# Row norms of a two-layer decoder trunk: turning by products with a diagonal of row scales instead of scaling and transposing

## The reference

```
def rms_norm(x, g):
    y = x * lax.rsqrt(jnp.mean(x * x, axis=-1, keepdims=True) + RMS_EPS)
    return y * g

mem_n = rms_norm(mem, mem_norm_g)
for layer in range(2):
    xn = rms_norm(h, norm_g[layer])
    mem_kv = mem_n @ mem_w_kv[layer]
    mixed = even_layer(xn, ...) if layer % 2 == 0 else odd_layer(xn, ...)   # begins with xn @ w_in
    h = h + mixed @ w_out[layer]
return rms_norm(h, final_norm_g)
```

## Time and profile before

| | before |
|---|---|
| median of 3 runs | 2272.27 us (2271.89 to 2274.04) |
| the profiled execution | 2272.63 us |
| its span in the profile | 2271.0 us |
| TensorE busy | 2232.5 us (98%) |
| VectorE, ScalarE, GpSimd busy | 1018.3, 821.7, 409.4 us |
| chain that ended last: TensorE | 96% |

### The profile page before, as it was taken

The page is one execution under the profiler, slowest core; times in us unless marked ns, Lnnn a source line. Parts: engine busy times, 40 slices in busy tenths (PEclk is TensorE's granted clock), DMA queues, the critical chain, the costliest instruction groups (busy, mean ns, idle before and its releaser), DMA issues.

```text
span 2271.0 us, 30508 instructions
## 1 busy us (share of the span) xinstructions
PE 2232.5 (98%) x11709; PEld 1820.8 (80%) x11709; DVE 1018.3 (45%) x1897; ACT 821.7 (36%) x1465; POOL 409.4 (18%) x699
## 2 busy tenths in 40 slices
PE   7999999999999999999999999999999999999998
PEld 7888888888888788888788778888887866787886
DVE  4632465555532356642453432441122256666534
ACT  6532233333323444422432223222322444555323
POOL 1626113222311012100000002000000253221100
PEclk9999999999999999999999999999999999999999
DMA  8645444444445346653434447345443664554632
GB/s 285 202 140 133 137 116 130 140 133 114 127 120 195 123 146 203 195 191 101 150 115 129 129 141 242 112 135 165 140 122 111 200 214 152 162 191 137 215 102 93
DMA packets 167050, 345.63 MB, mean 152 GB/s; under 512 B 21663, under 2 KB 32239, under 8 KB 164483
## 3 DMA queue, kind: packets, MB, share of 16 engines
q1 hardware_dynamic: 106832, 188.51, 27.9%
q0 software_dynamic: 31376, 98.44, 13.6%
q10 hardware_dynamic: 28707, 56.84, 6.8%
HBM read 279.89 MB, written 63.83 MB: 151 GB/s over the span
## 4 chain that ended last, share of the span: by engine, by line
PE 96%; ACT 1%; issue 1%; DVE 1%; DMA 1%; POOL 0%; SPq 0%; ACTq 0%; DVEq 0%; POOLq 0%
PE PS L241 79%; PE PS L1715 3%; PE PS L2381 2%; PE PS L1704 2%; PE PS L291 1%; PE PS L2278 1%; PE PS L558 1%; PE PS L1886 1%; PE PS L1464 1%; PE PS L2241 1%; PE PS L2030 1%; PE PS L2274 1%; PE PS L1911 1%; ACT wsp L203 0%; PE PS L1115 0%
## 5 line engine op out<-in xcount | busy, mean ns | idle before, releaser
L241 PE MATMUL PS<-A,wsp 128*128 128x512 f32 (+2 forms) x5184 | 1159.5, 383 | 1.5 <-ACT stage L344 1.2
L241 PEld LDWEIGHTS PS<-A,wsp 128*128 128x128 f32 (+1 forms) x5184 | 941.4, 188 | 198.1 <-issue 7.5
L210 DVE TENSOR_TENSOR wsp<-wraw,wsp 128x1024 fp32r<-128x1024 f32 (+1 forms) x358 | 433.0, 1210 | 948.8 <-ACT wsp L203 947.6
L241 PE MATMUL PS<-wsp,A 128*128 128x512 f32 x2928 | 751.9, 401 | 3.7 <-DVE stage L1786 1.8
L203 ACT ACTIVATE wsp<-wraw 128x1024 fp32r<-128x1024 f32 (+1 forms) x358 | 372.2, 1042 | 908.5 <-PE PS L241 878.5
L241 PEld LDWEIGHTS PS<-wsp,A 128*128 128x128 f32 x2928 | 532.0, 189 | 103.8 <-issue 9.2
L344 ACT ACTIVATE stage<-PS 128x512 f32<-128x512 f32 (+1 forms) x150 | 87.1, 587 | 128.5 <-PE PS L241 121.9
L1751 ACT ACTIVATE S<-PS 128x256 f32<-128x256 f32 (+3 forms) x160 | 62.9, 393 | 122.5 <-PE PS L1704 121.7
L1759 ACT ACTIVATE S<-PS,stats 128x256 f32<-128x256 f32 (+3 forms) x160 | 74.8, 467 | 74.5 <-DVE stats L1796 63.7
L1715 PEld LDWEIGHTS PS<-S 128*128 128x128 f32 x640 | 93.0, 191 | 10.2 <-issue 1.0
L1715 PE MATMUL PS<-S 128*128 128x128 f32 x640 | 94.3, 274 | 0.5 <-issue 0.5
(11 more groups left out here) (347 smaller groups left out, 1730.4 us busy)
## 6 DMA issues: line engine op xcount, KB each, us to landing
wraw<-in_even_w_in_dram SPq DMA_DIRECT2D x112, 512.0 KB, 3.7
wraw<-in_odd_w_in_dram SPq DMA_DIRECT2D x88, 512.0 KB, 3.6
wraw<-in_w_out_dram SPq DMA_DIRECT2D x80, 512.0 KB, 3.8
wraw<-in_mem_w_kv_dram SPq DMA_DIRECT2D x32, 512.0 KB, 4.3
yO<-stage ACTq DMA_DIRECT2D x12, 1024.0 KB
yE<-stage ACTq DMA_DIRECT2D x10, 1024.0 KB
S<-yO POOLq DMA_DIRECT2D x36, 256.0 KB, 3.5
hA<-stage ACTq DMA_DIRECT2D x8, 1024.0 KB
```

Of the source, the lines that this page charges most:

```text
L210: nc.vector.tensor_tensor(wsp[:, q, 1, :, 0:j["cols"]], wraw[:, q, :, 0:j["cols"]], wsp[:, q, 0, :, 0:j["cols"]].bitcast(F32), ALU.subtrac ...
L241: mm = nc.tensor.matmul(dst, lhs, rhs, start=(s == 0 and kk == 0 and i == 0), stop=(s == j["spc"] - 1 and kk == 1 and i == 2))
```

## The change

- The rows are no longer scaled. `dve_diag` multiplies the identity by r of a token tile, into `tC` (128x128 per tile), and the transpose with the identity becomes a product of the unscaled rows with this diagonal: rows turned and scaled at once. `tC`, `hrows` and the product are float32, without the transpose flag. All 160 are changed.
- The small chain has one step less: the sign and the factor 4 are put into the mean of squares, so that the last two steps are one `scalar_tensor_tensor`.
- First norm: the squares of a memory tile are shared, columns 0 to 1023 by ScalarE, 1024 to 2047 by VectorE (`dve_square`). The first weight slot is split in two halves (`act_first`, `dve_first`), and TensorE starts after block 0 and the first half.
- Third norm: the token tiles are taken in two halves h of 256 tokens. Blocks 0 to 3 of half 0 are turned inside `pe_rows_last`, before its last six products; the first two slots of O1 are multiplied by halves, 12 products of 128x256 per weight block, half and slot (`pe_half_slot`); blocks 0 to 3 of half 1 are turned between them.
- The tiles of the position bias move to the upper half of `S` (T5 = 8192), so that their loads wait for the squares of the last row, not for the store of h1; the load of c waits for the last bias stores, and the load of the compression inputs for the store of h1 and the last turned blocks.

```diff
         def pe_tile(pe, v, k):
-            if k == 0 or (k == 4 and v["k"] != 1):
-                pe.wait_ge(rows_ok, {(0, 0): 2, (0, 4): 3, (1, 0): 8, (2, 0): 11, (2, 4): 13}[v["k"], k])
...
+            if k == 0:
+                pe.wait_ge(diag_ok, (2, 6)[v["k"]])
...
-            rows = scaled if v["k"] == 2 else hrows
             for t in range(v["tiles"]):
-                mm = nc.tensor.transpose(PS[:, 4 + k % 4, t * P:(t + 1) * P], rows[:, t, k * P:(k + 1) * P], ident[:, :])
+                mm = nc.tensor.matmul(PS[:, 4 + k % 4, t * P:(t + 1) * P], hrows[:, t, k * P:(k + 1) * P], diag(t), start=True, stop=True)
             mm.then_inc(nt_pe, 1)
...
+        def dve_diag(dve, t):
+            nc.vector.tensor_scalar(diag(t), ident[:, :], small[:, 20 + t:21 + t], None, ALU.mult).then_inc(diag_ok, 1)
...
-            nc.vector.tensor_scalar(r1, r1, -0.5, 1.5, ALU.mult, ALU.add).then_inc(rms_step, 1)
-            dve.wait_ge(rms_step, step + 4)
-            nc.vector.tensor_tensor(r, r0, r1, ALU.mult).then_inc(row_root, 1)
+            nc.vector.scalar_tensor_tensor(r, r1, 3.0, r0, ALU.add, ALU.mult).then_inc(row_root, 1)
...
+        def dve_square(dve, t):
+
+            dve.wait_ge(mem_in[t], 16)
+            half = hrows[:, t, D // 2:D]
+            nc.vector.tensor_tensor_reduce(S[:, 14336 + 1024 * t:15360 + 1024 * t] if t == 0 else S[:, 12288:13312], half, half, -4.0 / D, -4.0 * EPS,
+                                           ALU.mult, ALU.add, accum_out=small[:, 2 + t:3 + t]).then_inc(sq_dve, 1)
...
+                    if f == 3 and s == j["spc"] - 1 and midway:
+                        midway()
...
+        def pe_half_tiles(pe, h):
+
+            pe.wait_ge(diag_ok, 8 + 2 * h)
+            for k in range(4):
+                bank, cs = half_bank(h, k)
+                for t in (2 * h, 2 * h + 1):
+                    o = cs.start + t % 2 * P
+                    mm = nc.tensor.matmul(PS[:, bank, o:o + P], hrows[:, t, k * P:(k + 1) * P], diag(t), start=True, stop=True)
+                if k % 2:
+                    mm.then_inc(half_pe, 1)
...
+        def pe_norm_halves(pe, v, j):
...
+            for kk in range(2):
+                pe_half_slot(pe, j, 0, 0, kk)
+            pe_half_slot(pe, j, 1, 0, 0)
+            pe_half_tiles(pe, 1)
+            pe_half_slot(pe, j, 1, 0, 1)
+            for kk in range(2):
+                pe_half_slot(pe, j, 0, 1, kk)
+            pe.wait_ge(half_lo, 8)
+            tiles(4)
+            for kk in range(2):
+                pe_half_slot(pe, j, 1, 1, kk)
+            tiles(6)
...
@@ the lists of the engines @@
-            pe_rows_last(pe, OUT0B, 3, 2)
-
-            pe_norm(pe, NORMS[2], O1)
+            pe_rows_last(pe, OUT0B, 3, 2, lambda: pe_half_tiles(pe, 0))
+            pe_norm_halves(pe, NORMS[2], O1)
...
+            dve_diag(dve, 0)
+            dve_diag(dve, 1)
             dve_out_row(dve, OUT0B, 3, 16, 2)
-            dve_part(dve, 0, 0, 1024)
+            for k in range(2):
+                dve_half_tile(dve, NORMS[2], 0, k)
             dve_out_row(dve, OUT0B, 3, 16, 3)
```

More of the change, by code:

```diff
@@ L211, in dve_slot, with pe_part @@
                                     wsp[:, q, 0, :, 0:j["cols"]].bitcast(F32), ALU.subtract).then_inc(w_lo, 1)
-        def pe_part(pe, j, c, s, n, q, free, bank, m0, m1):
+        def pe_part(pe, j, c, s, n, q, free, bank, m0, m1, waits=True):
             turned = j["mode"] == "T" or (isinstance(c, int) and c in j["turned"])
@@ L222, in pe_part @@
                 wp, ap = ((0, j["hi"]), (0, j["lo"]), (1, j["hi"]))[i]
-                if m == 0:
+                if m == 0 and waits:
                     pe.wait_ge(w_lo, n + 1)
@@ L388, in build @@
         junk = PS[:, 4:8, :]
-        NORMS = [dict(tiles=2, g=2, k=0), dict(tiles=4, g=0, k=1), dict(tiles=4, g=1, k=2, out=OUT0B, sq0=6, step0=10, root0=2, row0=0, rows=2),
-                 dict(tiles=4, k=3, out=OUT1B, sq0=22, step0=18, root0=4, row0=2, rows=1)]
-        scaled = S[:, 8192:16384].rearrange("p (t d) -> p t d", t=4)
+        NORMS = [dict(tiles=2, g=2, k=0), dict(tiles=4, g=0, k=1), dict(tiles=4, g=1, k=2, out=OUT0B, sq0=4, step0=8, root0=2, row0=0, rows=2),
+                 dict(tiles=4, k=3, out=OUT1B, sq0=20, step0=14, root0=4, row0=2, rows=1)]
         sqp = sb("sqp", [P, 4, 4])
@@ L524, in dve_rms @@
             nc.vector.reciprocal(r0, root).then_inc(rms_step, 1)
-            dve.wait_ge(rms_step, 5 * v["k"] + 2)
+            dve.wait_ge(rms_step, 4 * v["k"] + 2)
             nc.vector.tensor_tensor(r1, r0, r0, ALU.mult).then_inc(rms_step, 1)
-            dve.wait_ge(rms_step, 5 * v["k"] + 3)
+            dve.wait_ge(rms_step, 4 * v["k"] + 3)
             nc.vector.tensor_tensor(r1, r1, var, ALU.mult).then_inc(rms_step, 1)
[L529 to L536, removed]
+            dve.wait_ge(rms_step, 4 * v["k"] + 4)
+            nc.vector.scalar_tensor_tensor(r, r1, 3.0, r0, ALU.add, ALU.mult).then_inc(rows_ok, 1)
+            dve.wait_ge(rows_ok, v["k"] + 1)
         def dve_tile(dve, v, k):
@@ L570, in pe_norm @@
                 pe_tile(pe, v, k)
-            pe.wait_ge(nt_lo, KD * v["k"] + 2)
-            pe_chunk(pe, j, 0, following)
+            pe.wait_ge(nt_lo, KD * v["k"] + 1)
+            for s, n, q, r, early in chunk_slots(j, 0):
+                if s == 0:
+                    pe.wait_ge(first_lo, 1)
+                    pe_part(pe, j, 0, s, n, q, pe_free(j, 0)[0], 0, 0, 12, waits=False)
+                    pe.wait_ge(nt_lo, KD * v["k"] + 2)
+                    pe.wait_ge(w_lo, n + 1)
+                    pe_part(pe, j, 0, s, n, q, pe_free(j, 0)[0], 0, 12, 24)
+                else:
+                    pe_slot(pe, j, 0, s, n, q, pe_free(j, 0)[0])
+                following(s)
@@ new lines, in pe_half_slot @@
+        def pe_half_slot(pe, j, s, h, kk):
+            _, n, q, r, early = first_slots(j)[s]
+            pe.wait_ge(w_lo, n + 1)
+            pe.wait_ge(half_lo, 4 * h + 2 * s + kk + 1)
+            free = pe_free(j, 0)[0]
+            for f in range(4):
+                for i in range(3):
+                    if s == 0 and kk == 0 and i == 0 and h == 0:
+                        pe.wait_ge(banks_free, free[f])
+                    wp, ap = ((0, j["hi"]), (0, j["lo"]), (1, j["hi"]))[i]
+                    mm = nc.tensor.matmul(PS[:, f, 256 * h:256 * h + 256], wsp[:, q, wp, kk, f * P:f * P + P],
+                                          A[:, ap + 2 * s + kk, 256 * h:256 * h + 256], start=(s == 0 and kk == 0 and i == 0 and h == 0), stop=False)
+            if h == 1 and kk == 1:
+                mm.then_inc(slot_used, 1)
@@ new lines, in pe_norm_halves, with tiles @@
+        def pe_norm_halves(pe, v, j):
+            def tiles(k0):
+                for k in (k0, k0 + 1):
+                    if k < KD:
+                        pe_tile(pe, v, k)
+            for kk in range(2):
[7 more added lines that the diff above has]
+            tiles(4)
+            for kk in range(2):
+                pe_half_slot(pe, j, 1, 1, kk)
+            tiles(6)
+            for s, n, q, r, early in first_slots(j)[2:]:
+                pe.wait_ge(nt_lo, KD * v["k"] + 2 * s - 2)
+                pe_slot(pe, j, 0, s, n, q, pe_free(j, 0)[0])
+                tiles(2 * s + 4)
@@ L2075, in pool_c @@
         def pool_c(pool):
+            for r in range(2):
+                pool.wait_ge(t5_out[r], 16 * 16)
             pool.wait_ge(stored, 16 * (O1["stored0"] + 2))
@@ L2081, in pool_cmp @@
         def pool_cmp(pool):
-            for r in range(2):
-                pool.wait_ge(t5_out[r], 16 * 16)
+            pool.wait_ge(h1_out, 16)
+            pool.wait_ge(nt_pe, 3 * KD - 4)
             pool.wait_ge(stored, 16 * (O1["stored0"] + 5))
@@ L2626, in _ @@
             act_row_square(act, NORMS[2], 2)
-            act_part(act, 0, 1024, D)
+            for k in range(4):
+                act_half_tile(act, NORMS[2], 0, k)
             act_row_square(act, NORMS[2], 3)
             act_row_root(act, NORMS[2], 1)
[L2630 to L2633, removed]
+            for k in range(4):
+                act_half_tile(act, NORMS[2], 1, k)
             act_split(act, O1, 2)
@@ L2766, in _ @@
             dve_row_root(dve, NORMS[2], 0)
+            dve_diag(dve, 0)
+            dve_diag(dve, 1)
             dve_out_row(dve, OUT0B, 3, 16, 2)
-            dve_part(dve, 0, 0, 1024)
+            for k in range(2):
+                dve_half_tile(dve, NORMS[2], 0, k)
             dve_out_row(dve, OUT0B, 3, 16, 3)
-            dve_part(dve, 1, 0, 1024)
+            for k in range(2, 4):
+                dve_half_tile(dve, NORMS[2], 0, k)
             dve_row_root(dve, NORMS[2], 1)
[L2772 to L2775, removed]
+            dve_diag(dve, 2)
+            dve_diag(dve, 3)
+            for k in range(4):
+                dve_half_tile(dve, NORMS[2], 1, k)
             dve_split(dve, O1, 2)
```

131 lines of the change are left out of this document (77 added, 54 removed).

## The result

| | before | after |
|---|---|---|
| median of 5 runs | 2272.65 us (2271.89 to 2274.04) | 2283.76 us (2282.91 to 2286.97) |
| the profiled execution, its span | 2272.63, 2271.0 us | 2286.97, 2285.3 us |
| TensorE busy, records | 2232.5 us, 11709 | 2251.6 us, 11917 |

The changed kernel is slower: ratio 1.005 with a 95% interval of 1.0035 to 1.0064, 11.1 us between the medians, where 11.0 were forecast. The interval stays clear of 1, so the change costs some half a per cent.

A forecast was written before the change was run, and what follows sets the result against it. TensorE, busy for 98% of the span, bounds the kernel, so time is saved only where it waits. Terms 2.2 + 7.2 + 1.8 − 0.2 = +11.0 on 2272.63 give 2283.6, stated as 2283.5 us; range 2280.5 to 2287.

The forecast's parts named there:

- The price: All three norms: a diagonal float32 product takes two records, 0.222 us, twice a transpose's 0.11 us.
- The first norm's start: First norm up to its first weight products: TensorE starts 1.2 us earlier, changing the time by −0.5 us (−1.0 to +0.1).
- The half of the slow remainder: First norm's first 24 weight products: half of their 1.10 us of slow-pace excess was taken as saved.
- The loop and the second norm: First norm's six groups of four add +2.7 us; second norm's 16 groups, in busy TensorE's stream, add +7.2 us.
- The third norm: OUT0B to O1: wait and slow clock go, but 64 diagonal products and 96 half products cost more; +1.8 us.
- half 1's slack of 0.7: Third norm: half 1's small chain and diagonals done at 1121.1, 0.7 us before TensorE finishes three half slots.
- The end: Last row's chain at the kernel's end loses one step: −0.2 us.
- The bias tiles' move: Bias table loads no longer wait for the store of h1; set to 0, within half a microsecond either way.
- One record per product: Rival, all norms: a diagonal product costs only 0.11 us, so −6.8 us, 2265.8, faster; chance 0.05.
- Returned waits: Rival, third norm: slacks of 0.7 and 0.8 vanish through more, smaller handovers; 2287.5 with 2 of waits; chance 0.08.
- The rival's "over 3 us": Third norm: a TensorE wait over 3 us brings back the slow clock, 16 more records at 0.225, +1.8 us.
- Hidden extra: Rival, second norm: TensorE's added 7.2 us falls on splits that are late anyway; 2276; chance 0.04.

The follow-up runs named there:

- before_products: The kernel before with each of the 160 norm transposes made a plain float32 product with the identity, nothing moved; 2290.6 us (before 2273.14).
- turn_unscaled: The changed kernel with all 160 diagonal products turned back into transposes of the unscaled rows, row factor left out; 2265.85 us (before 2273.14).
- after_again: The changed kernel run once more, unchanged; 2283.44 us (before 2273.14).
- norm2_scaled: The changed kernel with the second norm as before: VectorE scales the four tiles, its 64 blocks are transposes; 2276.01 us (before 2273.14).
- no_halves: The changed kernel with the third norm in the order of before, whole slots, but diagonal products and no scaled rows; 2288.28 us (before 2272.7).
- halves_scaled: As mixed, but no diagonal at the third norm: those columns scaled by VectorE and ScalarE, turned by transposes; 2265.85 us (before 2272.7).
- mixed: The changed kernel with only 24 diagonal products, where TensorE used to wait; other rows scaled and transposed, bias tiles back; 2268.99 us (before 2272.7).

## Why the prediction was right

**The price** is the step that decides, and it held: two records of 0.111 us (320 records; 0.89 for four), read from a pair of helpers in attention that turn a block once and use it once. before_products and turn_unscaled show it from both sides, +17.5 and −17.6 us for 160 blocks, so 0.11 us for each second record.

**The first norm's start** (−0.5, bounds −1.0 to +0.1; measured −0.73): the first diagonal product was put at 11.85 and stands at 11.92; the squares on VectorE took 1.23 + 0.08, the two diagonals 0.49; the 16 slow records 3.78 against 3.6. The half of the slow remainder was a guess, and that it came out near is luck: with the same instructions at the start, the first 24 weight products take 2.88 us (here), 3.61 (after_again), 2.87 (norm2_scaled) and 3.90 (no_halves), and the first slot ends at 18.58, 19.09, 18.15 and 19.60, so from −1.16 to +0.29 against before. The bounds of −1.0 to +0.1 were too narrow, and the spread of 1.4 us belongs to the executions, not to the change.

**The loop and the second norm** (+2.7, +7.2; measured +2.71, +7.07): the stream of a busy TensorE pays everything, and norm2_scaled gives it back.

**The third norm** (+1.8; measured +1.69): half 0's diagonals, half 1's slack of 0.7 (diagonals ready at 1130.0, used at 1130.73) and the half products' 0.120 (36 in 4.31) were all as worked out. That a gain by the order (5.5 us in this stretch of turn_unscaled) and a loss by the price (48 + 16 second records, 7.1 us) stand against each other is seen in no_halves on the one side, halves_scaled on the other.

**The end** (−0.2): from TensorE's last product to the last row's scaling the chain takes 2.82 us in both profiles of the changed kernel, 3.01 before.

**The bias tiles' move** was set to 0; mixed and halves_scaled have them in the old place and reach what was expected within 0.7 us. It wasn't tried alone. Behind the third norm, to the end, the four profiles with moved tiles and no wait for kvD take 1109.0 to 1109.9 us, those two 1108.5 and 1108.6: a cost of half a microsecond or more isn't excluded.

**The rivals.** One record per product: its kernel, turn_unscaled, differs from the changed one in nothing but these 160 operations, and it is faster than before, so the price decides. That its time is the one worked out, 2265.85 for 2265.8, is in part luck, since the terms miss: the first norm gained 0.9 in its profile where 1.7 stood, as the slow products took the rest back, and the third 5.5 where 4.9 stood, with half a microsecond for a returned wait that didn't return. Returned waits: none at the reordered place, in this kernel's two profiles and the four experiments' that keep the halves. The rival's "over 3 us" isn't a measured threshold: waits of 3.6 and 4.1 us at the third norm were followed by the low level, but so was one of 1.9 us in the attention, with shorter gaps before it. Hidden extra: refuted by norm2_scaled. What I hadn't named is the low clock in the attention, 3.4 us in one execution; it is why the slowest run reached the top of the range.

**Wrong in size, in the experiments:** how long TensorE works at the low level behind a wait. For before_products I took the 3.6 us of the earlier trace rows; it was 6.0. For no_halves I took the norm of before_products over, and there it was 3.4.

## What to carry to other kernels

Before an operation is traded for another on the bound engine, look in the trace for a place that already has both, and divide records and chain time by the blocks: here a float32 product cost two transposes, and 160 second records outweighed a good reordering. Judge the parts of a change apart: turning and scaling in one product was the loss, filling the wait with the other half's products was the gain, and the gain alone is the faster kernel. A multiplication on engines that have time was free here, at the second norm and in the halves (norm2_scaled, halves_scaled), and taking it away from them bought nothing.

## What the runs showed of the hardware

- A float32 product of 128x128 by 128 columns is two records of 0.111 us, with a diagonal and with the identity as with full data; the zeros don't help.
- The granted clock fell to 0.50 (the 1.2 GHz level) in or behind a wait of TensorE and came back while it worked. Behind the wait of 4.1 us at the third norm TensorE worked at 0.50 for 3.4 us (before) and for 6.0 us (before_products). Behind that of 3.6 us (no_halves) it first worked for 1.4 us at 1.00 and then for 3.4 us at 0.50. Half of the slow time is what it costs, an estimate of 1.7 to 3.0 us for waits of nearly one length.
- In the attention of one execution, TensorE was busy for 2.27 of 4 us, with a wait of 1.9 us for a DMA load at the end, and then worked at 0.50 for 6.8 us, which cost 3.4 us (13.36 instead of 9.99 for the same products). The load's wait and the low clock did not occur in the next profile of the same kernel.
- At the start of the kernel the view gives 1.00 while the records take twice their time (16 in 3.78 us); there only the durations show the slow level. How much slow work is left for the weight products there differs by 1 us between executions with the same instructions.
- VectorE's sum of squares of 128x1024 float32 (a product with accumulation) took 1.23 us and 0.08 for the read of its sum, as long as the tensor_tensor of that size in the earlier trace rows.
